# Eight gate tiles of the first mixing stage, made in the last two bodies of the first heads' stage

## What is computed

```python
z, xbc, dt_raw, hq, hf, hi, hg, gate_s, gate_h = split(h @ w_in)
y_ssd = ...   # first heads: from z, xbc, dt_raw
y_hg  = ...   # second heads: from hq, hf, hi, hg
mix = sigmoid(gate_s) * (y_ssd @ w_ssd_br) + sigmoid(gate_h) * (y_hg @ w_hg_br)
x = x + mix @ w_out
```

## Time and profile before

| | us |
|---|---|
| median of 3 runs | 5006.86 (5006.2 to 5008.29) |
| the profiled execution | 5005.71 |
| its span, first to last instruction | 5003.9 |
| TensorE busy | 4865.2 |
| VectorE busy | 3167.1 |
| ScalarE busy | 1689.4 |
| GpSimd busy | 1059.0 |

### The profile page before, as it was taken

One profiled execution on the slowest core, in us unless ns is written; L12 is line 12 of the kernel. 1 busy time (PEld: TensorE's weight loads), 2 busy tenths in 40 slices (PEclk: granted clock), 3 DMA queues, 4 the chain that ended last, 5 costly groups with the idle time before them and its releaser, 6 DMA issues. The chain is left out here.

```text
span 5003.9 us, 65592 instructions
## 1 busy us (share of the span) xinstructions
PE 4865.2 (97%) x24160; PEld 4199.5 (84%) x24160; DVE 3167.1 (63%) x4253; ACT 1689.4 (34%) x1740; POOL 1059.0 (21%) x425
## 2 busy tenths in 40 slices
PE   8999969999999999999989999999999899999998
PEld 6777758888887787887879999999999788888887
DVE  5666658878888100101038866666767599888888
ACT  3223223333333322222232348875222222222221
POOL 2333310000000344443334430001322011111110
PEclk9999989999999999999999999999999999999999
DMA  3222212222221333334323357778998799888885
GB/s 123 80 84 88 80 59 87 80 80 80 82 80 65 128 113 113 141 126 166 114 92 116 113 213 281 277 279 305 336 341 327 278 338 319 307 305 308 299 300 204
DMA packets 238757, 913.95 MB, mean 183 GB/s; under 512 B 18400, under 2 KB 109152, under 8 KB 160608
## 3 DMA queue, kind: packets, MB, share of 16 engines
q1 hardware_dynamic: 201824, 644.63, 36.6%
q0 software_dynamic: 36864, 268.45, 14.7%
HBM read 837.78 MB, written 75.24 MB: 182 GB/s over the span
## 5 line engine op out<-in xcount | busy, mean ns | idle before, releaser
L195 POOL TENSOR_TENSOR ring_low<-ring_raw,ring_high 128x2048 fp32r<-128x2048 f32 x165 | 767.5, 4652 | 2181.9 <-ACT ring_high L190 2181.9
L213 PE MATMUL rt_acc<-h_high,ring_high 128*128 128x384 f32 (+1 forms) x2304 | 792.1, 344 | 15.0 <-DVE h_low L231 12.3
L214 PE MATMUL rt_acc<-h_low,ring_high 128*128 128x384 f32 (+1 forms) x2304 | 785.7, 341 | 0.0
L215 PE MATMUL rt_acc<-h_high,ring_low 128*128 128x384 f32 (+1 forms) x2304 | 785.4, 341 | 0.0
L190 ACT ACTIVATE ring_high<-ring_raw 128x2048 fp32r<-128x2048 f32 x336 | 643.6, 1916 | 380.5 <-PE out_acc L215 127.8
L213 PEld LDWEIGHTS rt_acc<-h_high,ring_high 128*128 128x128 f32 x2304 | 433.6, 188 | 30.2 <-issue 9.8
L215 PEld LDWEIGHTS rt_acc<-h_high,ring_low 128*128 128x128 f32 x2304 | 433.4, 188 | 10.5
L214 PEld LDWEIGHTS rt_acc<-h_low,ring_high 128*128 128x128 f32 x2304 | 433.6, 188 | 9.3
L213 PE MATMUL hg_acc<-h_high,ring_high 128*128 128x512 f32 x1024 | 408.3, 399 | 9.6 <-DVEq L1025 9.6
L215 PE MATMUL hg_acc<-h_high,ring_low 128*128 128x512 f32 x1024 | 401.1, 392 | 0.0
L214 PE MATMUL hg_acc<-h_low,ring_high 128*128 128x512 f32 x1024 | 399.7, 390 | 0.0
(11 more groups left out here) (319 smaller groups left out, 9950.6 us busy)
## 6 DMA issues: line engine op xcount, KB each, us to landing
ring_raw<-u_tiles SPq DMA_DIRECT2D x128, 1024.0 KB, 5.5
ring_raw<-v_tiles SPq DMA_DIRECT2D x128, 1024.0 KB, 6.6
ring_raw<-w_hg SPq DMA_DIRECT2D x64, 1024.0 KB, 4.8
ring_raw<-w_ssd SPq DMA_DIRECT2D x48, 1024.0 KB, 4.7
ring_raw<-w_mix_s SPq DMA_DIRECT2D x32, 1024.0 KB, 4.8
ring_raw<-w_mix_h SPq DMA_DIRECT2D x32, 1024.0 KB, 4.8
gelu<-sb_rt_gelu SPq DMA_DIRECT2D x128, 192.0 KB, 5.1
gates<-gate_table SPq DMA_DIRECT2D x12, 2048.0 KB, 7.7
```

The source lines that it names most:

```text
L195: nc.gpsimd.tensor_tensor(ring.low[:, slot], ring.raw[:, slot], ring.high[:, slot].bitcast(F32), ALU.subtract).then_inc(ring.low_ready, 1)
L213: nc.tensor.matmul(out, high[:, m], x_high[:, k, tokens], start=(k == 0), stop=False, skip_group_check=True)
L214: nc.tensor.matmul(out, high[:, m], x_low[:, k, tokens], start=False, stop=False, skip_group_check=True)
L215: last = nc.tensor.matmul(out, low[:, m], x_high[:, k, tokens], start=False, stop=(k == KT - 1), skip_group_check=True)
```

## The change

Of the first mixing stage's 16 gate tiles, the last eight (EARLY = 8, for n = 8 to 15) are computed in the two last bodies of the first heads' stage: six in body G, two in body G+1. For each, SP loads the weight tile, ScalarE and GpSimd split it, TensorE does the product in the two halves of a step, ScalarE applies tanh into `half_tanh`, and SP stores that to a new DRAM tensor `gates_s`. Two slots of `half_tanh` are used in turn, and the tanh of gate i waits for the store of gate i-2. In body G+1 the sum of squares moves between the halves of the product. In the mixing stage, bodies 0 to 7 are as before; bodies 8 to 15 (unrolled) have the branch product alone, into `acc[n % 2]`; SP reads the stored tanh into `before`, and VectorE makes the gate from it. Other stages are as before, but for their place in the ring.

```diff
+EARLY = 8
+LATE = KT - EARLY
@@ ssd_stage
+        EXTRA = {G: SSD_TILES, G + 1: EARLY - SSD_TILES}
+        early = lambda u, s: s < EXTRA.get(u, 0) if type(u) is int else False
@@ SP
-            load_ahead(sp, ring, G * SSD_TILES, following)
+
+            def load_gate(i):
+                load_tile(sp, ring, i % 2, dram["w_mix_s"][2 * (LATE + i)], G * SSD_TILES + i)
+
+            def store_gate(i):
+                sp.wait_ge(gate_read, i + 1)
+                sp.dma_start(gates_out[i], half_tanh[:, i % 2]).then_inc(gate_stored[i % 2], 16)
+
+            for i in range(4):
+                load_gate(i)
+            store_gate(0)
+            load_gate(4)
             store(G - 2)
+            store_gate(1)
+            load_gate(5)
+            for i in range(6, EARLY):
+                store_gate(i - 4)
+                load_gate(i)
+            store_gate(EARLY - 4)
+            store_gate(EARLY - 3)
+            load_ahead(sp, ring, G * SSD_TILES + EARLY, following)
+            store_gate(EARLY - 2)
             store(G - 1)
+            store_gate(EARLY - 1)
@@ ScalarE
-                    if proj and not (first and s == 0):
+                    if (proj or early(u, s)) and not (first and s == 0):
                         split_high(nc, act, ring, (s + 1) % 2, SSD_TILES * u + s + 1, 3 * u + (s + 1) // 2)
...
+                    if early(u, s):
+                        i = SSD_TILES * (u - G) + s
+                        act.wait_ge(ring.used, ring.base + SSD_TILES * u + s + 3)
+                        if i < 2:
+                            act.wait_ge(sig_done, SSD_TILES * G + 2)
+                        else:
+                            act.wait_ge(gate_stored[i % 2], 16 * (i // 2))
+                        nc.scalar.activation(half_tanh[:, i % 2], acc[s % 2][:], ACT.Tanh,
+                                             scale=0.5).then_inc(gate_read, 1)
                     if s == 1 and fin:
                         act.wait_ge(summed, f + 1)
@@ TensorE
-                    if proj:
+                    if proj or early(u, s):
                         pe.wait_ge(ring.low_ready, ring.base + n + 1)
-                        pe.wait_ge(acc_read, n + 1)
+                        i = 0 if proj else SSD_TILES * (u - G) + s
+                        if i < 2:
+                            pe.wait_ge(acc_read, n + 1)
+                        else:
+                            pe.wait_ge(gate_read, i - 1)
                         half(0)
                     if s == 0 and fin:
                         part_b(f, NC - 1)
+                    if s == 1 and fin and not comp:
+                        sum_squares()
...
-                    if proj:
+                    if proj or early(u, s):
                         half(1).then_inc(ring.used, 1)
@@ mix_stage
+        late = LATE if gates is not None else KT
+        TILES = late + KT
@@ SP
+            def load_late(sp):
+                for n in range(late, KT):
+                    load_tile(sp, ring, n % 2, w[2 * n + 1], n + late)
+                    sp.wait_ge(gate_ready, n + 1)
+                    sp.dma_start(before[:], gates[n - late]).then_inc(before_landed, 16)
+                    if n - 2 >= late - 1 and n < KT:
+                        store(n - 2)
@@ ScalarE
+            for n in range(2 * late, TILES):
+                split_high(nc, act, ring, n % 2, n, n // 2)
@@ TensorE
+            def late_body(n):
+                pe.wait_ge(ring.low_ready, ring.base + n + late + 1)
+                if n == late:
+                    pe.wait_ge(gate_tanh, late)
+                else:
+                    pe.wait_ge(mixed_ready, n - 1)
+                product(nc, acc[n % 2][:], ring.high[:, n % 2], ring.low[:, n % 2], y_high, y_low
+                        ).then_inc(ring.used, 1)
@@ VectorE
+            def late_body(n):
+                dve.wait_ge(before_landed, 16 * (n - late) + 16)
+                dve.wait_ge(mixed_ready, n)
+                nc.vector.tensor_scalar(gate[:], before[:], 1.0, 0.5, ALU.add, ALU.mult).then_inc(gate_ready, 1)
+                dve.wait_ge(gate_ready, n + 2)
+                dve.wait_ge(ring.used, ring.base + n + late + 3)
+                dve.wait_ge(stored, 16 * n)
+                nc.vector.tensor_tensor(mixed[:], acc[n % 2][:], gate[:], ALU.mult).then_inc(mixed_ready, 1)
```

More of the change, by code:

```diff
@@ L382, in ssd_stage @@
         y_stored = sem("y_stored")
+        gate_read = sem("gate_read")
+        gate_stored = [sem("gate_stored0"), sem("gate_stored1")]
+        EXTRA = {G: SSD_TILES, G + 1: EARLY - SSD_TILES}
+        early = lambda u, s: s < EXTRA.get(u, 0) if type(u) is int else False
         act_done = sem("act_done")
@@ L408, in _ @@
                 store(u - 2)
-            load_ahead(sp, ring, G * SSD_TILES, following)
-            store(G - 2)
+            def load_gate(i):
[7 more added lines that the diff above has]
+            load_gate(4)
+            store(G - 2)
+            store_gate(1)
[7 more added lines that the diff above has]
+            store_gate(EARLY - 2)
             store(G - 1)
+            store_gate(EARLY - 1)
+            for i in range(2):
+                sp.wait_ge(gate_stored[i], 16 * (EARLY // 2))
             sp.wait_ge(y_stored, 32 + 32 * G)
@@ L417, in _ @@
             split_low(nc, pool, ring, 0, 2)
-            with pool.Fori(1, G * SSD_TILES // 2) as i:
+            with pool.Fori(1, (G * SSD_TILES + EARLY) // 2) as i:
                 for n in (1, 2):
@@ L558, in half, with sum_squares @@
                                        range(i * KT // 2, (i + 1) * KT // 2))
-                    if proj:
-                        pe.wait_ge(ring.low_ready, ring.base + n + 1)
-                        pe.wait_ge(acc_read, n + 1)
+                    def sum_squares():
+                        pe.wait_ge(squared, f + 1)
+                        pe.wait_ge(decayed, NC * f + NC + 1)
+                        for t in range(2):
+                            last = nc.tensor.matmul(ps_decay[:], const["ones"], y_sq[:, t],
+                                                    start=(t == 0), stop=(t == 1))
+                        last.then_inc(summed, 1)
+                    if proj or early(u, s):
+                        pe.wait_ge(ring.low_ready, ring.base + n + 1)
+                        i = 0 if proj else SSD_TILES * (u - G) + s
[3 more added lines that the diff above has]
+                            pe.wait_ge(gate_read, i - 1)
                         half(0)
@@ L574, in body @@
                     if s == 1:
[L575 to L581, removed]
+                        if fin and comp:
+                            sum_squares()
                         if comp:
@@ L777, in _ @@
             body(G + 1, False, False, True)
-    ring.base += G * SSD_TILES
+    ring.base += G * SSD_TILES + EARLY
 def hg_stage(nc, dram, ring, h, const, y_out, following):
@@ L1188, in hg_stage, with mix_stage @@
     ring.base += H * HG_TILES
-def mix_stage(nc, name, w, ring, h, y_src, prior, dst, following, split=None):
+def mix_stage(nc, name, w, ring, h, y_src, prior, dst, following, gates=None, split=None):
     with ExitStack() as ctx:
@@ L1240, in load_mixed @@
                              dst[tiles].rearrange("k p t -> p k t")).then_inc(m_landed[i % 4], 16)
-            with sp.Fori(0, KT - 1) as n:
+            with sp.Fori(0, late - 1) as n:
                 for s in range(2):
@@ L1246, in _ @@
                 store(n)
-            load_prior(KT - 1)
+            load_prior(late - 1)
+            if gates is not None:
+                load_late(sp)
             if split is None:
-                load_ahead(sp, ring, 2 * KT, following)
-                store(KT - 1)
+                load_ahead(sp, ring, TILES, following)
+                for n in range(max(late - 1, KT - 2), KT):
+                    store(n)
                 sp.wait_ge(stored, 16 * KT)
@@ L1263, in _ @@
         def _(pool):
-            split_low_all(nc, pool, ring, 2 * KT)
+            split_low_all(nc, pool, ring, TILES)
         @block.scalar
@@ L1283, in mixed_high @@
                                      ACT.Copy).then_inc(m_high_ready, 1)
-            with act.Fori(0, KT - 1) as n:
+            with act.Fori(0, late - 1) as n:
                 tanh(n)
@@ L1288, in _ @@
                 split_high(nc, act, ring, 1, 2 * n + 3, n + 1)
-            tanh(KT - 1)
+            tanh(late - 1)
+            for n in range(2 * late, TILES):
+                split_high(nc, act, ring, n % 2, n, n // 2)
             if split is not None:
@@ L1312, in body @@
                         wait_piece=(lambda i: pe.wait_ge(y_low_ready, i)) if first else None).then_inc(ring.used, 1)
+            def late_body(n):
[6 more added lines that the diff above has]
+                        ).then_inc(ring.used, 1)
             body(0, True)
-            with pe.Fori(1, KT) as n:
+            with pe.Fori(1, late) as n:
                 body(n, False)
+            for n in range(late, KT):
```

(15 more changed lines are left out.)

7 lines of the change are left out of this document (4 added, 3 removed).

## The result

| | before | after |
|---|---|---|
| median of the runs, us | 5006.53 (4 runs) | 4968.84 (4967.48 to 4972.49, 4 runs) |
| the profiled execution, us | 5005.71 | 4969.47 |
| its span, us | 5003.9 | 4967.7 |

The ratio is 0.9927 with a 95% interval of 0.9915 to 0.9939: 0.7% faster, small but clear of no change; 36.2 us lie between the two profiled executions. On another chip the changed kernel gave 0.9935 (0.9921 to 0.9948).

The account below looks back on a forecast made before the run. TensorE, busy 97% of the span, was taken as the bound, idle mainly in the drain. -87.0 (mixing stage) + 51.2 (later next stage) = -35.8 us, giving 4969.9 profiled and a 4971.0 us median, range 4965 to 4978.

Parts of the forecast that it names:

- Eight products at 10.88 us, -87.0: Mixing stage: eight products leave it, each 10.88 us, shortening it by 87.0 us if late bodies stay bound by TensorE.
- Bodies G and G+1, product 55 done at 774.4: First heads' stage: body G lasts a full body's 80.27 us; product 55's last matmul in G+1 ends at 774.4.
- The tail, next stage at 786.5: After product 55: tanh, table load, logarithm to y_norm, stores, stage change; next stage starts at 786.5, 51.2 us later.
- The clock at the next stage's start: Second heads' stage: its slow first matmuls stay, saving none of the 1.9 us; bounds -1.9 and +1.
- Rival 1: Bodies G, G+1: GpSimd's low parts stop VectorE; 35.3 us, no gain (0.02), or in part +8.8, 4979.8 (0.06).
- Rival 2: The unrolled bodies: splits don't keep up, TensorE waits 2.66 us in 4 of 16 products; +10.6, 4981.6; chance 0.05.
- the straight code: Unrolled last two and late bodies, some 800 matmuls: cost taken as 0, bounded by -1 and one 2.66 us wait.
- Rival 3: Mixing stage: single buffers pace the late bodies; gain gone at 15.4 us a body, 5058 at 21.76; chance 0.03.
- Rival 4: Tail of first heads' stage: logarithm's table loaded before the tanh, -1.3, 4969.7; 4967.8 with the clock; no separate chance.

Follow-up runs that it names:

- yardstick: The changed kernel run once more, unedited, beside the first follow-up edits: 4972.75 us against 5004.46 before the change.
- two reads: Changed kernel, each late body of the mixing stage reading its gate twice, one read after the other has landed: 4974.04 us.
- six tiles: Changed kernel with EARLY = 6: only six gate tiles moved, all into body G, none in body G+1: 4979.56 us.
- ten tiles: Changed kernel with EARLY = 10: ten gate tiles moved, six in body G and four in body G+1: 4967.19 us.
- five reads: Changed kernel, each late body of the mixing stage reading its gate five times, one after another: 5014.36 us, ratio 1.0018 to before.
- the run without low parts: Changed kernel, GpSimd making only 16 of 2048 columns of the low part for seven of the eight gate tiles: 4969.84 us.
- the early sum and the early root together: Changed kernel, ScalarE making the last norm's root before the last tanh, sum of squares still between the product's halves: 4966.46 us, again 4965.93.
- the early root alone: Changed kernel, root before the last tanh, but sum of squares put back behind product 55: 4970.41 us.

## Why the prediction was right

It said 4971.0 us (4965 to 4978); 4968.84 was measured. For the profiled execution it said 4969.9; 4969.47. The mechanism held link by link, but that the sum is right within half a microsecond is in part luck: the mixing stage gave 1.8 us more than said, and the tail (0.4) and the two other rows of the table above (0.5 each) took 1.4 of that back. As the bullets show, most of these are scatter between executions.

- **Eight products at 10.88 us, -87.0.** The mixing stage became 88.8 us shorter. The late bodies have exactly the pace predicted; the further 1.8 us are in the stage's head. From the stage's first matmul to ScalarE's second table load it was 41.6 us before (1632.00 to 1673.57) and 39.8 after (1684.17 to 1723.95), but 41.9 in the yardstick's trace of the same kernel and 42.2 with two reads. So it isn't the change, but scatter between executions of one kernel, and two things in it can be read. TensorE's waits for y's low parts sum to 2.3 us before, 1.6 after and 1.8 in the yardstick. And the granted clock differs. The stage starts with 11 slow matmuls before and 7 in both others, some 0.8 us; and behind a wait of 3.0 us for a weight tile's low part the matmuls go on at 0.23 us in the changed kernel's trace, while in the yardstick's eight of them stand 0.43 apart, 1.6 us more. In the order of time, first the changed kernel, then the yardstick:

```profile
1712.68 0.50 PE L215 MATMUL mix_s_acc<-h_high,ring_high 128*128 128x512 f32 x1 [2.96 <-POOL ring_low L197]
...
1714.85 0.39 PE L215 MATMUL mix_s_acc<-h_high,ring_high 128*128 128x512 f32 x1
```

```profile
1713.38 0.50 PE L215 MATMUL mix_s_acc<-h_high,ring_high 128*128 128x512 f32 x1 [3.00 <-POOL ring_low L197]
...
1715.32 0.63 PE L216 MATMUL mix_s_acc<-h_low,ring_high 128*128 128x512 f32 x1
```

  Over the nine traces with eight moved tiles and undisturbed late bodies (all but those of six tiles, ten tiles and five reads) the mixing stage takes 272.6 to 276.4 us, 274.6 in the mean, against 361.5 before: 86.9 shorter. There is one trace of the kernel before, so that figure is good to some 2 us.
- **Bodies G and G+1, product 55 done at 774.4.** The last tanh starts at 774.53. That a body filled with six products would last as long as a full one was the step with most weight, and it held within 0.2 us: 666.71 to 746.81, from the last tanh of the loop to that of body G, is 80.1.
- **The tail, next stage at 786.5.** 786.91. Mis-sized is the price of the third store and the semaphores: 0.5 was said, and 0.93 is what the rows show, 780.54 to 786.72 against 729.83 to 735.08. Where the gate's store alone is last, it takes 4.8 from its issue (774.96 to 779.74), with the new semaphores there too.
- **The clock at the next stage's start**, taken as unchanged: 14 slow matmuls, 786.91 to 793.02, instead of 9, some 1.0 us, at the edge of the bound. This is scatter too: of the traces whose two last bodies are the same, those of the yardstick, of the low parts left out and of two reads have 13 or 14 slow matmuls, and that of five reads has 6.
- **Rival 1** (GpSimd in VectorE's way): the hold is real and its price is nothing, by the run without low parts. That it becomes dear as soon as the hold is twice as long shows how much of the cover it uses; 5.08 against 0.70 us for one and the same operation shows the hold itself. The Trainium skill's exclusive lock ("SBUF — State Buffer", SBUF: two separate sides) agrees with these two rows. What decided here was the cover.
- **Rival 2**, and the straight code, taken as 0: the only wait from 670 to 774 us is the 0.8 us for a VectorE copy. None is for a low part. (In the first unrolled body the longest idle row is 5.92 us, at the stage's first matmul, for VectorE's split of h, and not the 2.66; that none ends with TensorE's own instructions stands.)
- **Rival 3**: the chain was put at 3.8 to 4.2 us and the point of no gain at 15.4 us a body. The chain is longer than that: between the read of the next gate and the weight load a store lands after 3.2 us in the median rather than 2.0 to 2.4, so from the multiply (1887.14) over the store's issue (1888.76) it is 4.8 us. The term was small against the 10.88 us that cover it, and so this cost nothing. Both sides were tried: one more read fits, four more give 16.5 to 17.1 us and a kernel slower than before.
- **Rival 4** named 1.3 us for a table loaded sooner and didn't see what ScalarE's order was worth: 6.8 us, because the whole of the norm's chain could lie beside product 55 and the last store would be the gate's alone. It was in the rows: the sum was to be done by 768.8, and the logarithm put at 776.4.

## What to carry to other kernels

A stage that drains pays for its idle engine twice, in time and in clock; independent products from a later stage fill it at the price of a full body, and nothing more is won once TensorE is busy to the end, as the run with ten tiles shows. Price the moved work by a full body's period, then look at what has come to stand last in each queue: here one activation put ahead of a long chain cost 7 us. And what is moved for such a chain may pay only in pairs: the early sum and the early root together brought 5.0 us, the early root alone 0.2, and the early sum alone cost 1.8. Before single buffers take over a stage's pace, work out their chain and compare it with the product that covers it.

## What was not expected of the hardware

A wait of 3.6 us on TensorE in the middle of a busy stretch was enough for the granted clock to fall to its lower level, 1.2 GHz: 11 matmuls stood 0.44 us apart before 2.4 GHz was back, so the 3.6 us cost 5.9. A wait of 3.0 us did so in some executions and not in others: it stands in the mixing stage's head in all 13 traces of this case, and behind it 8 matmuls were slow in four of them, 13 in two and none in seven. The changed kernel's two traces fall on either side. That is 1.6 to 2.6 us, a good part of the 5 us by which runs of one kernel differ. From 670 to 774 us, where the one wait is 0.8 us, the granted clock stayed at 1.00.

A 256 KB store landed later beside other transfers: the store of `mixed` took 2.0 us in the mixing stage before the change, and 3.2 in the late bodies, where a read of 256 KB is issued 0.4 us ahead of it and a load of 1 MB 0.5 us behind. The last of these stores, with neither, took 2.0 again. Which of the two neighbours costs the 1.2 us wasn't tried.
